# Constant matmuls without a reader at the end of the first mixer and before the odd mixer's gating matmuls

## What is computed

```python
# gated delta branch, its end (per head pair p in the kernel)
o = o * lax.rsqrt(jnp.mean(o * o, axis=-1, keepdims=True) + EPS) * norm_w
o = o * jax.nn.silu(z)
...
mix = jnp.concatenate([att, ssd, gdn], axis=-1) @ w_out[l]

# odd mixer, its gating (8 groups, 4 blocks of 128 tokens)
v = layer_norm(jax.nn.gelu(v).reshape(bsz, seq, G_C, HEAD_DIM), sgu_g)
mix = jnp.einsum('gts,bnsgd->bntgd', jnp.tril(sgu_w), v) + ...
o_c = u * mix.reshape(bsz, seq, C_WIDTH)
```

## Time and profile before

| | us |
|---|---|
| runs, median (lowest, highest) | 1921.59 (1919.95, 1921.93) |
| the profiled execution's own time | 1919.31 |
| its span, first to last instruction | 1917.5 |
| TensorE busy in the span | 1871.7 (98%) |
| mean granted TensorE clock | 0.994 |

### The profile page before, as it was taken

How to read it: one execution, slowest core, us unless ns; L and a number is a source line. 1 busy time by engine, 2 the same in 40 slices (tenths; PEclk the granted TensorE clock), 3 DMA queues, 4 the chain that set the end, 5 groups by cost and what they waited for, 6 DMA issues and landing times.

```text
span 1917.5 us, 23337 instructions
## 1 busy us (share of the span) xinstructions
PE 1871.7 (98%) x9766; PEld 1543.5 (80%) x9766; DVE 978.7 (51%) x1555; ACT 727.4 (38%) x1223; POOL 251.8 (13%) x170
## 2 busy tenths in 40 slices
PE   7999988999999999999999999999999999999998
PEld 7788977888888888777788888888778888888886
DVE  5675555232322254776565655522654565555334
ACT  5664434232322243556724434321323244344211
POOL 1433410111110023211000111100000001111000
PEclk9999999999999999999999999999999999999999
DMA  5211032223232232101022232332322322322321
GB/s 198 68 54 67 7 133 67 88 89 109 88 110 96 91 124 83 66 30 38 23 88 89 90 108 88 107 124 77 110 88 89 110 71 106 104 95 89 120 99 66
DMA packets 28765, 170.02 MB, mean 89 GB/s; under 512 B 3386, under 2 KB 5602, under 8 KB 10866
## 3 DMA queue, kind: packets, MB, share of 16 engines
q1 hardware_dynamic: 28660, 168.53, 25.6%
HBM read 166.37 MB, written 2.11 MB: 88 GB/s over the span
## 4 chain that ended last, share of the span: by engine, by line
PE 90%; DVE 7%; ACT 1%; issue 1%; DMA 0%; POOL 0%; SPq 0%; DVEq 0%; ACTq 0%
PE ps L572 26%; PE ps L573 26%; PE ps L574 26%; PE ps L1112 2%; PE ps L1040 1%; DVE wL L1812 1%; PE ps L1075 1%; PE ps L1079 1%; PE ps L1097 1%; DVE x L2352 1%; DVE x L2347 1%; DVE hL L1819 1%; PE ps L702 1%; PE ps L652 1%; PE ps L856 0%
## 5 line engine op out<-in xcount | busy, mean ns | idle before, releaser
L572 PE MATMUL ps<-hH,wH 128*128 128x512 f32 (+1 forms) x1568 | 604.2, 385 | 7.8 <-DVE hL L1819 4.8
L573 PE MATMUL ps<-hL,wH 128*128 128x512 f32 (+1 forms) x1568 | 592.2, 378 | 0.0
L574 PE MATMUL ps<-hH,wL 128*128 128x512 f32 (+1 forms) x1568 | 592.2, 378 | 0.0
L1812 DVE TENSOR_TENSOR wL<-raw,wH 128x1024 fp32r<-128x1024 f32 (+2 forms) x250 | 304.0, 1256 | 379.5 <-ACT wH L1281 379.5
L1281 ACT ACTIVATE wH<-raw 128x1024 fp32r<-128x1024 f32 (+2 forms) x298 | 290.2, 1023 | 283.7 <-PE ps L574 283.6
L572 PEld LDWEIGHTS ps<-hH,wH 128*128 128x128 f32 x1568 | 297.1, 189 | 69.0 <-issue 5.5
L574 PEld LDWEIGHTS ps<-hH,wL 128*128 128x128 f32 x1568 | 296.9, 189 | 54.5
L573 PEld LDWEIGHTS ps<-hL,wH 128*128 128x128 f32 x1568 | 297.4, 190 | 52.5 <-issue 1.4
L572 PE MATMUL ps<-wH,aH 128*128 128x512 f32 x528 | 209.0, 396 | 0.0
L573 PE MATMUL ps<-wL,aH 128*128 128x512 f32 x528 | 208.8, 395 | 0.0
L574 PE MATMUL ps<-wH,aL 128*128 128x512 f32 x528 | 208.8, 395 | 0.0
(11 more groups left out here) (370 smaller groups left out, 1900.4 us busy)
## 6 DMA issues: line engine op xcount, KB each, us to landing
raw<-in_wbig SPq DMA_DIRECT2D x139, 1024.0 KB, 4.8
rows<-in_rows SPq DMA_DIRECT2D x12, 512.0 KB, 5.7
x<-in_x SPq DMA_DIRECT2D x8, 512.0 KB, 5.6
raw<-in_wbig SPq DMA_DIRECT2D x8, 512.0 KB, 3.6
out<-x SPq DMA_DIRECT2D x4, 512.0 KB, 2.6
near<-u_scratch SPq DMA_DIRECT2D x1, 1024.0 KB, 7.3
raw<-in_wbig SPq DMA_DIRECT2D x1, 1000.0 KB, 7.7
raw<-in_wbig SPq DMA_DIRECT2D x1, 600.0 KB, 10.4
```

What stands on the lines that cost most here:

```text
L572: e.matmul(o, hi, m_hi, start=first, stop=False)
L573: e.matmul(o, hi, m_lo, start=False, stop=False)
L574: return e.matmul(o, lo, m_hi, start=False, stop=end)
L1812: e.tensor_tensor(wL[r][:, cs], raw[r][:, cs], wH[r][:, cs].bitcast(F32), ALU.subtract).then_inc(*low_dve.one(c, h))
```

## The change

A helper issues n matmuls of `ones` with `ones` into a given slice of a bank. It is called with 18 in the end step of each half of the delta branch, between `clear(a)` and the wait for `og`, and in each gating step, between the wait for `sgw` and the first wait for `vn`: 18 at j = 0, 6 at j = 1, 2 and 3. The real work that follows in the same step overwrites the bank's slice (`start=True`). 36 matmul calls are added at each of the two sites; nothing is removed or moved.

```diff
+            def keep_warm(o, n):
+                w.wait_ge(*pre.dve.at("ones"))
+                for _ in range(n):
+                    e.matmul(o, ones[:, :], ones[:, :], start=True, stop=True)
+
...
                 yield
                 clear(a)
+                keep_warm(ps[a][:, 0:128], 18)
                 w.wait_ge(*gdn[p].dve.at("og"))
                 for i in range(4):
                     m = e.transpose(ps[a][:, 128 * i:128 * i + 128], ogz[p][:, i, :], ident[:, :])
...
                 for j in range(4):
                     clear(j)
                     w.wait_ge(*odd.pool.at("sgw"))
+                    keep_warm(ps[j][:, 0:128], 18 if j == 0 else 6)
                     for n in range(4):
                         w.wait_ge(*odd.dve.at("vn", n))
```

## The result

The changed kernel takes 1925.93 us, the median of 13 runs (1924.39 to 1928.55), against 1921.59 us before (13 runs, 1919.95 to 1923.82). The ratio is 1.0023, with a 95% interval of 1.0015 to 1.0032: slower by about 4.3 us, where 2.1 us was forecast. The measured time lies in the range, and the sign is as forecast. The profiled execution took 1924.64 us, with a span of 1922.8 us; that is 5.3 us more than the one of before.

What follows compares the result with a forecast made beforehand. TensorE, busy for 98% of the span, was taken to bound the kernel, its pauses also lowering the clock. Mixer's end +0.65, first gating step -2.5, other three +4.0 gave +2.1 us, 1923.7 against the median 1921.59; range 1919.4 to 1927.4.

Steps and rivals of the forecast that it cites:

- rival (b): First gating step: the clock falls all the same in the pauses left, +4.65 us, so 1926.2; chance 0.12.
- the forecast's own upper bound of +4.1 us: Whole kernel: the sum if each constant-matmul instruction takes 0.13 us, +1.9 - 2.5 + 4.7.
- the prediction's border of 3.8 us: Whole kernel: about 0.2%, what a measurement can tell from no change; same 0.75, slower 0.20, faster 0.05.
- The price of a pass: Both sites: each fp32 constant-matmul instruction takes 0.112 us, so 18 calls 4.0 us and 6 calls 1.34 us.
- Rival (c): Both sites: passes cost 0.064 us since the stationary tile never changes, -2.6 us, so 1919.0; chance 0.12.
- Rival (a): Both sites: the clock does not hold under constant matmuls, +10.9 us, so 1932.5; chance 0.08.
- the -2.5: First gating step: passes hide in VectorE's pace, the clock holds, and step j = 1 begins 2.5 us sooner.
- the +4.0: Other three gating steps: no pause there, so all 36 instructions lie on the path, 3 x 1.34 = 4.0 us.
- -2.1 of dense work regained: Projection behind the mixer's end: at full clock its first 13 matmuls win back 2.1 us of the +2.75 later start.
- Rival (d): Both sites: slow-clock stretches are longer in typical runs, each regains 1 to 1.2 us more, sum about -0.2; chance 0.1.
- +0.65 us: Mixer's end, net: start of the projection +2.75 us, dense work regained -2.1 us.
- I cost all of these at nothing: Behind the mixer's end: late `end` signals, `hL`, chunk 14's parts and the `x` reload cost 0, covered by chunk 13's 10 us.

Runs made afterwards that it cites:

- guard_after: The changed kernel with one more wait, so GpSimd's product of `sgw` starts only after VectorE's low part of chunk 102: 1924.43 us, ratio 1.0018 against before.
- control: The kernel before, unchanged, run and traced again: ratio 0.9995 (0.9986 to 1.0004).
- after: The changed kernel with all its constant matmuls, against the kernel before: 1925.93 us, ratio 1.0023.
- after_again: The changed kernel once more, unaltered, for a second trace: mixer's end 24.56 us, gating stage 22.69 us; no whole time is given.
- a_only: The kernel before with only the two sets of 18 calls at the mixer's end, none in the gating steps: ratio 1.0014 (1.0005 to 1.0023).
- start_fill: The kernel before with 36 small constant matmuls (72 instructions) in TensorE's first wait, nothing at the mixer's end: ratio 1.0004 (0.9995 to 1.0013).

## Why the prediction was right, and where its size was off

**That the time lies in the range** is in part luck. The range reached to 1927.4 for rival (b), which did not occur; the forecast's own upper bound was +4.1 us, and 4.3 were measured. By the prediction's border of 3.8 us the result is "slower by more", to which it gave 0.20, and not "same", 0.75.

**The price of a pass** was right: 0.112 us in each of 36 instructions, and 1.34 us for each set of 12 (4.0 for the three in the gating stage). Rival (c), a cheaper pass for a tile that never changes, is out. The 81 ns of the Trainium skill's page "TensorE: Matmul & The Clock Gate" (Back-to-back issue gap) does not hold for fp32 passes here, as line 702's rows had said.

**The clock under constant matmuls.** Rival (a) is out: 1.00 from 257.4 to 270.2 and from 1428.7 to 1452. Values that are all ones hold the clock like others. With this the Trainium skill ("TensorE: Matmul & The Clock Gate", Part 1) agrees. Rival (b) is out: 0.89 us of wait were left in the first gating step and the clock stayed, as it did in all seven traces with the 18 calls there; in all six without them it fell.

**The odd mixer's gating stage** was right in each term: the -2.5 measured as -2.3 us by the ratio, the +4.0 as 22.70 - 18.67 = 4.0 us in the traces. VectorE set the pace of the first step, so the 18 calls cost nothing there. Without a set the stage took 21.1 to 21.2 us in four traces and 20.16 in two, 20.8 in the mean, so the gain of the first set is 2.1 us in the mean and 2.5 at most, and the stage's net +1.9 instead of +1.5.

**The mixer's end** came out too good. That the projection began at 267.36, with 267.45 forecast, is luck: by the forecast it begins 20.38 us behind the wait for `wT` (17.63 + 2.75), and it began 21.22 us behind it, after an early fall, in an execution that reached that wait 0.93 us sooner. Without an early fall (`guard_after`) it was 20.02. The step that failed is "-2.1 of dense work regained". It took the clock's stretch of one execution as that of all. From the first matmul to the 13th the projection took 4.89 us there, but 3.34 to 4.89 in the seven traces without a set, 3.90 in the mean, and 2.85 with the full set: 1.05 us regained, half of 2.1. Rival (d) thought of longer stretches than the one shown, which would have made the change cheaper; the control had a shorter one, and in nine of the 13 traces the clock had already fallen before the last steps of the mixer (as at 254 above), so that these ran slowly whether constant matmuls followed or not. Over the traces, the mixer's end takes 22.69 us without a set (seven) and 23.99 with the full set (after, after_again, a_only, guard_after): +1.3 us, not +0.65. Some of this is an uneven share of early falls: among traces without one it is +1.0 us (21.86 to 22.87), among those with one also +1.0 (23.32 to 24.36).

**The term that was missing** is as large as the odd mixer's net. Where the prediction says "I cost all of these at nothing", it followed semaphores and queues behind the mixer's end, and did not count that TensorE's program becomes longer. With 72 matmuls and 72 weight loads more, the packet of the instruction queue comes 16 us ahead of SyncE's load of `sgg` and no longer beside it; `sgw` lands sooner, and GpSimd's product meets VectorE's low part. The wait of 1.66 us stood in both traces of the changed kernel; over the whole stretch the meeting cost 1.95. With 76 or 144 instructions added ahead the load was issued in 0.33 us in seven of seven traces, and the two met in five of five without the guard; `start_fill` shows that the site of the instructions does not matter. That the packet carries TensorE's program is shown by the counts (one packet for every 256 of its instructions). Why a packet slows the issue of a load is not shown.

The sum as the traces have it: +1.0 to 1.3 at the mixer's end, +1.9 in the gating stage, +1.95 for the meeting, 4.9 to 5.2 in all, against 4.3 (2.9 to 6.1) measured.

## What to carry to other kernels

Fill a pause of TensorE with constant matmuls only as far as it is idle, and put none where it has no pause: 18 calls in VectorE's shadow gave 2.3 us, three times 6 calls in none took 4.0. What a fall of the clock costs at one place needs more than one trace, since stretches at half speed came and went between executions of the same kernel; compare traces that fell alike. And where two engines pass each other by 2 us, an edit elsewhere can let them meet; a wait that orders them cost nothing measurable here (0.9997, 0.9988 to 1.0006).

## What was not expected of the hardware

The number of instructions in TensorE's program shifts the load issue of SyncE. With a packet of the instruction queue 0.45 to 0.59 us ahead, SyncE's load took 0.80 to 1.29 us to issue, and 0.33 without, in 13 of 13 traces (the one where two loads were swapped counts for the load that came first). A packet alone does not do it. In the 13 traces 62 loads that stood by themselves began within 1.2 us behind such a packet, and all were issued in 0.33 to 0.34 us. The 11 that followed another load within 1.5 us, with a packet 0.45 to 1.05 us ahead, all took longer: these six, and five of `rows` near 955 us, 0.48 to 0.72 us instead of 0.43.

VectorE's 128x1024 subtraction of two SBUF tiles and GpSimd's 128x1024 product took turns. Whichever began first kept its own time (1.21 or 1.22 us for a half, 2.34 for the product), and the other ended 1.08 or 1.09 us (a half) or 2.23 to 2.26 us (the product) behind it, in all ten traces in which they overlapped.
